# Latent norm and rotary steps on PSUM sources, the second attention's projections ahead, and levels 1 to 4 of a blocked triangular inverse on 32x32 blocks

## The reference

```python
x = x + 0.5 * swiglu(rms_norm(x, ffa_norm), ffa_w_in, ffa_w_out)
h = rms_norm(x, mix_norm)
c_q, c_kv, k_rope, g_q, g_k, g_v, g_b, g_a, g_z, m_qkv, gate_logits = split_cols(h @ w_in, IN_SPLITS)
# mla: latent norm, up projections, norm of each head, rotary turn, causal attention
q = rms_norm((rms_norm(c_q, cq_norm) @ w_uq).reshape(b, s, 8, 96), q_norm)
kv = (rms_norm(c_kv, ckv_norm) @ w_ukv).reshape(b, s, 8, 128)
# gdn: short convolution, l2 norm, then in chunks of 64 a unit lower triangular solve
sol = triangular_solve(eye + a, rhs, lower=True, unit_diagonal=True)
# moba: the second attention, 8 heads of 64
q = rope(rms_norm(q, q_norm), pos); k = rope(rms_norm(k, k_norm), pos)
x = x + sum(sigmoid(gate_logits) * (branches @ w_branch)) @ w_out
x = x + 0.5 * swiglu(rms_norm(x, ffb_norm), ffb_w_in, ffb_w_out)
```

## Time and profile before

| | |
|---|---|
| median of 3 runs | 2693.65 us (2691.25 to 2694.6) |
| the profiled execution | 2696.59 us, span 2694.8 us |
| PE busy | 2490.3 us, 92% of the span |
| DVE, ACT, POOL busy | 903.2, 901.4, 1022.9 us |
| mean granted TensorE clock | 0.965 |
| layer 1 | some 1166 to 1928 us of the span |
| layer 2 | some 1928 to 2692 us of the span |

### The profile page before, as it was taken

The page is one execution under the profiler, slowest core; times in us unless marked ns, Lnnn a source line. Parts: engine busy times, 40 slices in busy tenths (PEclk is TensorE's granted clock), DMA queues, the critical chain, the costliest instruction groups (busy, mean ns, idle before and its releaser), DMA issues. The chain is left out here.

```text
span 2694.8 us, 37867 instructions
## 1 busy us (share of the span) xinstructions
PE 2490.3 (92%) x15110; PEld 1793.4 (67%) x15110; DVE 903.2 (34%) x1374; ACT 901.4 (33%) x1310; POOL 1022.9 (38%) x428
## 2 busy tenths in 40 slices
PE   8879999999999999869998899899699988999999
PEld 3544443443343344349987799799699877998998
DVE  0331221221221122152147765321331287563211
ACT  1212111111111111134446533444344466523443
POOL 0000000000000000038866445688488675437786
PEclk9979999999999999879999899999899998999999
DMA  8139999999999999535544233455355443224453
GB/s 353 63 149 424 428 428 427 428 428 427 428 428 428 428 428 428 224 119 193 186 143 141 83 110 119 141 192 184 122 199 185 150 144 126 94 79 165 164 186 135
DMA packets 95100, 653.78 MB, mean 243 GB/s; under 512 B 10544, under 2 KB 12768, under 8 KB 68992
## 3 DMA queue, kind: packets, MB, share of 16 engines
q1 hardware_dynamic: 94976, 652.06, 62.8%
HBM read 650.96 MB, written 1.06 MB: 242 GB/s over the span
## 5 line engine op out<-in xcount | busy, mean ns | idle before, releaser
L502 POOL TENSOR_TENSOR w_lo<-raw,w_hi 128x1024 fp32r<-128x1024 f32 (+2 forms) x424 | 1022.7, 2437 | 1654.7 <-ACT w_hi L496 1654.7
L1764 PE MATMUL bank<-ring,scratch 128*64 128x512 f32 x3072 | 686.1, 596 | 28.6 <-DMA ring<-in_expert_units 26.3
L515 PE MATMUL bank<-hT_hi,w_hi 128*128 128x256 f32 x1984 | 568.7, 287 | 18.4 <-issue 13.4
L496 ACT CAST w_hi<-raw 128x1024 fp32r<-128x1024 f32 (+2 forms) x424 | 421.3, 1039 | 477.1 <-PE bank L517 440.0
L516 PE MATMUL bank<-hT_lo,w_hi 128*128 128x256 f32 x1984 | 565.0, 285 | 0.0
L517 PE MATMUL bank<-hT_hi,w_lo 128*128 128x256 f32 x1984 | 564.9, 285 | 0.0
L1764 PEld LDWEIGHTS bank<-ring,scratch 128*64 128x64 f32 x3072 | 209.5, 137 | 456.7 <-issue 387.0
L515 PEld LDWEIGHTS bank<-hT_hi,w_hi 128*128 128x128 f32 x1984 | 384.3, 194 | 21.3 <-issue 17.0
L516 PEld LDWEIGHTS bank<-hT_lo,w_hi 128*128 128x128 f32 x1984 | 384.2, 194 | 1.2 <-issue 0.5
L517 PEld LDWEIGHTS bank<-hT_hi,w_lo 128*128 128x128 f32 x1984 | 383.9, 194 | 0.0
L1932 DVE TENSOR_TENSOR scratch<-bank,scratch 128x512 f32<-128x512 f32 x64 | 44.3, 692 | 605.9 <-PE bank L1778 602.0
(11 more groups left out here) (309 smaller groups left out, 2803.0 us busy)
## 6 DMA issues: line engine op xcount, KB each, us to landing
ring<-in_expert_units SPq DMA_DIRECT2D x192, 2048.0 KB, 20.6
raw<-in_layer_halves SPq DMA_DIRECT2D x408, 512.0 KB, 4.1
ring<-in_first_units SPq DMA_DIRECT2D x6, 2048.0 KB, 24.1
ring<-in_ple_units SPq DMA_DIRECT2D x2, 2048.0 KB, 9.8
raw<-in_layer_halves SPq DMA_DIRECT2D x8, 424.0 KB, 3.4
scratch<-in_norm_gains SPq DMA_DIRECT2D x6, 512.0 KB, 5.2
raw<-in_layer_halves SPq DMA_DIRECT2D x4, 384.0 KB, 3.3
const<-in_const SPq DMA_DIRECT2D x1, 1184.0 KB, 7.3
```

The lines of the kernel that those rows point to most:

```text
L496: k.nc.scalar.copy(k.w[0][i % SPLIT_SLOTS][:, at], k.raw[n % RAW_SLOTS][:, 0:at.stop - at.start]).then_inc(k.sem("weights_hi"), 1)
L502: k.nc.gpsimd.tensor_tensor(k.w[1][i % SPLIT_SLOTS][:, at], k.raw[n % RAW_SLOTS][:, 0:at.stop - at.start], k.w[0][i % SPLIT_SLOTS][:, at], ...
L515: nc.tensor.matmul(out, lhsT[0], rhs[0], start=start, stop=False)
L1764: last = nc.tensor.matmul(b[g * SL:(g + 1) * SL, :], lhsT[:, c, :], w[:, c, g, :], start=start and c == 0, stop=stop and c == 3)
```

## The change

- **Latent norm.** DVE no longer copies the `mla` rows to SBUF. ACT squares from the bank, and DVE scales and copies from the bank; only 8 columns are still copied (`G.ab`). The weight slot of `("mla", 0)` is given back after its last product, not with `("mla", 1)`.
- **Rotary steps.** Three banks (2, 6, 7) are lent to DVE (`lend`, `borrow`): the tables are copied into one, the products x1 s1 and x2 s2 go to the other two, so that each tensor_tensor of `rope_dve` has one source in SBUF and one in PSUM. `moba` is done in two groups, q and k.
- **Order.** `moba` q and k are projected before `raw(0,1)`; their norms and rotary steps follow those of `mla` at once on DVE, and three waits for a root (`head_root_act`) now stand between ACT's casts. `z` 0 comes before `values_pe`, `gates(1,3)` after the second `out_turned_pe`.
- **Inverse.** In levels 1 to 4 the inverse has only 32x32 blocks on its diagonal. `Xc` and `XTc` hold these blocks side by side, 32 columns a head; a level is 8 products m_block Xc with 32 columns, a mask that spreads them to 128, 8 products with XTc, a subtract and a 32x32 block transpose on DVE (no `XP`). One of the four parts of `gates(2,0)`, 12 matmuls of 256 columns, stands between `P` and `PX` of each. Level 4 ends with a spread and a transpose to full size; levels 5 and 6 are as before. `first_level_pe` and `first_level_act` go.

```diff
-MIX_HALVES = [("mla", 0), ("mla", 1), ("gdn", 1, 0), ("gdn", 1, 1), ("gdn", 0, 0), ("up", 0), ("up", 1), ("gdn", 0, 1),
-              ("moba", 0, 0), ("moba", 0, 1), ("moba", 1, 0), ("moba", 1, 1), ("gdn", 2, 0), ("gdn", 2, 1),
+MIX_HALVES = [("mla", 0), ("mla", 1), ("gdn", 1, 0), ("gdn", 1, 1), ("gdn", 0, 0), ("up", 0), ("up", 1),
+              ("moba", 0, 0), ("moba", 0, 1), ("moba", 1, 0), ("moba", 1, 1), ("gdn", 0, 1), ("gdn", 2, 0), ("gdn", 2, 1),
...
+def rope_tables_to_bank(k, dve, link, a):
+
+    b, full, _free = k.borrow(dve, ("rope", a.n, 0))
+    dve.wait_ge(k.sem("rope_tables"), a.n + 1)
+    words = 4 * 2 * NT * a.half
+    k.nc.vector.tensor_copy(b[:, 0:words], a.flat).then_inc(full, 1)
...
+    c1, s2, c2, s1 = (bc(table[:, j, r0:r1].unsqueeze(2), [P, r1 - r0, H, a.half]) for j in range(4))
+    first = V_.tensor_tensor(tmp[0], x1, s1, ALU.mult)
+    second = V_.tensor_tensor(tmp[1], x2, s2, ALU.mult)
...
+def compact_pe(k, pe, lev, between):
...
+        for h in range(GH):
+            last = nc.tensor.matmul(b[:, h * BLOCK:(h + 1) * BLOCK], G.m_block[:, t, h, :], G.Xc[:, GH * t + h, :], start=True, stop=True)
...
+    next(between)
...
+        for h in range(GH):
+            last = nc.tensor.matmul(b[:, h * BLOCK:(h + 1) * BLOCK], G.P[:, t, h, :], G.XTc[:, GH * t + h, :], start=True, stop=True)
...
+def compact_dve(k, dve, link, lev):
...
+        V_.tensor_tensor(grid(G.P[:, t]), spread(part(b, GH, BLOCK)), bc(level, [P, GH, P // BLOCK, BLOCK]), ALU.mult).then_inc(free, 1)
...
+        V_.tensor_tensor(G.XTc[:, at], G.XTc[:, at], part(b, GH, BLOCK), ALU.subtract).then_inc(free, 1)
+        k.evacuated(dve, ("PX", lev, t))
+        if lev < COMPACT:
+            V_.transpose(G.Xc[:, at].rearrange("p a n -> p (a n)"), G.XTc[:, at].rearrange("p a n -> p (a n)")).then_inc(k.sem("x_turned"), 1)
+        else:
+            link(V_.tensor_tensor(grid(G.XT[:, t]), spread(G.XTc[:, at]), block_mask(G), ALU.mult))
+            V_.transpose(G.X[:, t].rearrange("p h n -> p (h n)"), G.XT[:, t].rearrange("p h n -> p (h n)")).then_inc(k.sem("x_turned"), 1)
...
-            whole(raw_pe(k, pe, 0, 1), moba_part[0])
-            next(moba_part[1])
+            whole(moba_part[0], moba_part[1], raw_pe(k, pe, 0, 1))
             transposed_pe(k, pe, mla)
...
-            for lev in range(1, LEVELS):
+            between = gates_pe(k, pe, 2, 0)
+            for lev in range(1, COMPACT + 1):
+                compact_pe(k, pe, lev, between)
+            for lev in range(COMPACT + 1, LEVELS):
                 level_pe(k, pe, lev)
-            whole(gates_pe(k, pe, 2, 0))
...
-            whole(*[gates_pe(k, pe, 1, q) for q in range(4)])
+            whole(*[gates_pe(k, pe, 1, q) for q in range(3)])
             out_turned_pe(k, pe, 1)
+            whole(gates_pe(k, pe, 1, 3))
...
-                    ins = V_.tensor_scalar(cn[:, t, c0:c1], rows[:, t, c0:c1], latent[:, i, t:t + 1], None, ALU.mult)
+                    ins = V_.tensor_scalar(cn[:, t, c0:c1], b[:, c0:c1], latent[:, i, t:t + 1], None, ALU.mult)
...
+            rope_tables_to_bank(k, dve, link, mla)
+            rope_dve(k, dve, link, mla, 0)
+            rope_tables_to_bank(k, dve, link, moba)
+            for g in range(2):
+                head_variance_dve(k, dve, link, moba, g)
+                head_scale_dve(k, dve, link, moba, g)
+                rope_dve(k, dve, link, moba, g)
```

More of the change, by code:

```diff
@@ new lines, in rope_tables_to_bank, with rope_dve @@
+def rope_tables_to_bank(k, dve, link, a):
[3 more added lines that the diff above has]
+    k.nc.vector.tensor_copy(b[:, 0:words], a.flat).then_inc(full, 1)
+    dve.wait_ge(full, k.uses.at["rope", a.n, 0][1] + 1)
+def rope_dve(k, dve, link, a, g):
+    V_, (r0, r1) = k.nc.vector, a.groups[g]
+    table = k.bank[k.uses.at["rope", a.n, 0][0]][:, 0:4 * 2 * NT * a.half].rearrange("p (j r f) -> p j r f", j=4, f=a.half)
+    if g == 0:
+        lent = [k.borrow(dve, ("rope", a.n, 1 + j)) for j in range(2)]
+    tmp = [k.bank[k.uses.at["rope", a.n, 1 + j][0]][:, :].rearrange("p (r h f) -> p r h f", h=H, f=a.half) for j in range(2)]
+    rows = a.qk.rearrange("p (r h) d -> p r h d", h=H)[:, r0:r1]
+    x1, x2 = rows[:, :, :, a.rope_at:a.rope_at + a.half], rows[:, :, :, a.rope_at + a.half:a.rope_at + 2 * a.half]
+    c1, s2, c2, s1 = (bc(table[:, j, r0:r1].unsqueeze(2), [P, r1 - r0, H, a.half]) for j in range(4))
+    first = V_.tensor_tensor(tmp[0], x1, s1, ALU.mult)
+    second = V_.tensor_tensor(tmp[1], x2, s2, ALU.mult)
+    if g == 0:
+        for j, ins in enumerate((first, second)):
+            ins.then_inc(lent[j][1], 1)
+    V_.tensor_tensor(x1, x1, c1, ALU.mult)
+    last = V_.tensor_tensor(x2, x2, c2, ALU.mult)
+    if g == len(a.groups) - 1:
+        last.then_inc(k.bank_free[k.uses.at["rope", a.n, 0][0]], 1)
+        k.evacuated(dve, ("rope", a.n, 0))
+    else:
+        link(last)
+    third = V_.tensor_tensor(x1, x1, tmp[1], ALU.subtract)
+    fourth = V_.tensor_tensor(x2, x2, tmp[0], ALU.add)
+    if g == len(a.groups) - 1:
+        third.then_inc(k.bank_free[k.uses.at["rope", a.n, 2][0]], 1)
+        fourth.then_inc(k.bank_free[k.uses.at["rope", a.n, 1][0]], 1)
+    else:
+        fourth.then_inc(k.sem("qk_ready"), 1)
@@ new lines, in lower_dve @@
+    for q in range(P // BLOCK):
+        at = slice(q * BLOCK, (q + 1) * BLOCK)
+        ins = V_.tensor_tensor(G.XTc[at], G.m.rearrange("p t h n -> p (t h) n")[at, :, at],
+                               bc(first[at, at].unsqueeze(1), [BLOCK, NT * GH, BLOCK]), ALU.mult)
+    link(ins)
+    link(V_.tensor_tensor(G.XTc, bc(G.identc.unsqueeze(1), [P, NT * GH, BLOCK]), G.XTc, ALU.subtract))
+    V_.transpose(G.Xc.rearrange("p a n -> p (a n)"), G.XTc.rearrange("p a n -> p (a n)")).then_inc(k.sem("x_turned"), 1)
@@ L2045, in layer_uses @@
     turned = [("qkT", q, t, half) for q, t in QKT for half in range(2)]
-    add(*[(("qkT", 0) + key[1:], b) for key, b in zip(turned, (2, 6, 7, 3, 4, 2, 6, 7))])
+    add(*[(("qkT", 0) + key[1:], b) for key, b in zip(turned, (1, 3, 4, 5, 1, 3, 4, 5))])
+    add((("raw", 2, 0), 1))
     add((("score", 0, 0, 0), 3), (("score", 0, 0, 1), 4))
-    add(*[(("score", 0, 1, g), b) for g, b in enumerate((2, 6, 7, 3))])
-    add((("raw", 2, 0), 1), (("raw", 2, 1), 4))
-    add((("pT", 0, 0, 0), 5), (("pT", 0, 0, 1), 0), (("ss",), 2), (("moba", 2, 0), 6), (("moba", 2, 1), 7))
@@ L2058, in layer_uses @@
-    add((("gates", 0, 0), 0), (("gates", 0, 1), 1))
+    add(*[(("score", 0, 1, g), b) for g, b in enumerate((5, 2, 6, 7))])
+    add((("raw", 2, 1), 0), (("moba", 2, 0), 3), (("moba", 2, 1), 4))
+    add((("pT", 0, 0, 0), 5), (("pT", 0, 0, 1), 2), (("ss",), 6))
+    add(*[(("pT", 0, 1, g), b) for g, b in enumerate((7, 5, 2, 7))])
+    add((("z", 0), 1), (("z", 1), 0), (("oT", 0, 0), 5), (("oT", 0, 1), 2))
+    add(*[(("qkT", 1) + key[1:], b) for key, b in zip(turned, (7, 6, 3, 4, 7, 6, 3, 4))])
@@ L2140, in _ @@
                         lnorm_pe(k, pe, 1, 1)
+                    if t == 1 and h == 0:
+                        last.then_inc(k.sem("half_used"), 1)
                 last.then_inc(full, 1)
```

257 lines of the change are left out of this document (141 added, 116 removed).

## The result

The changed kernel takes 2651.13 us, the median of 4 runs (2647.76 to 2652.72), where the kernel before takes 2693.94 us beside it. The ratio is 0.9839, 95% interval 0.9826 to 0.9851: 43 us less, where 37 were forecast. The profiled execution took 2647.76 us, the fastest of the four, with a span of 2645.6 us; against the 2694.8 us of before that is 49 us, so a sum of parts from the traces runs some 3 us a layer above what the medians say.

What follows compares the result with a forecast made beforehand. PE, busy 92% of the span, bounds the kernel, through waits, half clock and work. Terms summed to -18.5 us a layer, -37 for two: 2696.6 to 2659.6 us, median 2.9 lower, 2656.7 us; range 2638 to 2682 us.

Steps and rivals of the forecast that it cites:

- start: Latent norm up to the up projections: waits of 1.58 and 5.49 us and 2.1 us of half clock go; -9.2 us.
- middle: First attention's rotary steps and roots: 6.3 us of waits go, new waits of 2.9 and 5.0 and 1.7 clock come; +3.3 us.
- second attention's rotary steps: Ahead of the second attention's transposes: the 9.06 us wait and its half clock go, one wait grows; -9.9 us.
- inverse and clock in it, with the turning: Compact levels 1 to 4, levels 5 and 6, saved turning of `X`: -5.8 us; a third of compact levels' time lost to clock: +6.6.
- end: After the second `out_turned_pe`: `gates(1,3)` covers the turned output's way over ACT and DVE; -3.5 us.
- Right in both waits: PE's waits of 1.58 us for a weight half and 5.49 us ahead of the up projections were to go.
- The two new waits: PE was to wait 2.9 us for `moba(1,1)`'s weights and some 5 us for ACT to empty the first turned bank.
- The one more half-clock stretch: In the middle, the new waits of 3 and 5 us were to bring one more stretch at half clock, +1.7 us.
- as slow with PSUM as now: Rival: rotary operations gain nothing from PSUM, about 13 us return on DVE, PE sees perhaps 8; 2673 us, chance 0.05.
- the wait that was to grow from 1.26 to 2.5 us: PE's wait in the second attention, as ACT takes `moba` 2 ahead of the last probabilities' copies; about 2.5 us.
- the waits behind level 4: Inverse: PE waits for each tile's spread and full-size transpose, and for a POOL piece; +3.0 us.
- products which bring few columns cost the clock: In the four compact levels, few-column products lower PE's clock as waits do; +6.6 us, bounds 0 and +19.9.

Runs made afterwards that it cites:

- start_alone: Kernel before with only the latent-norm part of the change and `gate_logits_dve` moved behind `cT`; 2682.75 us, ratio 0.9948.
- copies_first: Changed kernel with ACT's copies of the first attention's turned q and k ahead of a convolution tap and two weight casts; 2644.04 us.
- cast_first: Changed kernel with the cast of `moba(1,1)`'s weights ahead of the decay's exponentials and the first root on ACT; 2652.53 us.
- sbuf_rotary: Changed kernel with rotary tables read from SBUF and the first attention's products kept in SBUF too; 2684.87 us, ratio 0.9953.
- wide_products: Changed kernel with each product in levels 1 to 4 moving 128 columns, its head's 32 four times over; 2639.93 us.
- wide_lengths: Changed kernel with the 16 products of `lengths_pe` moving 128 columns of ones instead of two; 2654.17 us.
- gates_behind: Changed kernel with all four parts of `gates(2,0)` behind level 6 instead of one in each compact level; 2652.54 us.
- gate_after_level4: Changed kernel with the fourth part of `gates(2,0)` moved from the middle of level 4 to behind its last product; 2642.53 us.
- old_end: Changed kernel with all four `gates(1,q)` parts ahead of the second `out_turned_pe` again; 2658.64 us, ratio 0.9853.

## Why the prediction came out right, and where it was off

The measured terms are of layer 2, from the starts of the stages' first matmuls in the two traces. In the middle the one block of 5.5 us that came from the next stretch, half of the second attention's v, is counted where it was.

| term | forecast | measured |
|---|---|---|
| start | -9.2 | -10.2 (47.19 to 36.97 us) |
| middle | +3.3 | -0.2 |
| second attention's rotary steps | -9.9 | -10.9 |
| inverse and clock in it, with the turning | -5.8 + 6.6 = +0.8 | +0.05 (+0.90 - 0.85) |
| end | -3.5 | -4.0 |
| sum | -18.5 | -25.2 |

**Start.** Right in both waits: L2455 at 0.47 us, and nothing ahead of the up projections. `start_alone` shows the term by itself. The cause is right in the main: scaling and copying `cn` and the rotary columns took DVE 12.4 us before and 2.1 us now. The 3.9 us of the moved `gate_logits_dve` were not in the prediction, and no run has the one without the other.

**Middle.** This is the term that was mis-sized, by 3.5 us. The two new waits came as described, behind the first root and behind the third. The `w_lo` wait was 2.38 us for 2.9. The wait for ACT was 2.74 us for "some 5 us". Its chain was right: from the second root to the third 8.84 us (forecast 9), then a tap and a cast, 2.9 us (forecast 3). But the second root came 8.1 us before the end of `raw(0,1)` and not 6, and that shortened the wait. L819 was taken at 3.36 us and took 4.49. The one more half-clock stretch came as forecast: the changed kernel has two of 3.4 us between the decay and the scores, the kernel before has one. `copies_first` and `cast_first` show that both waits hang on the roots in ACT's queue.

**Rotary steps.** Right. L841 to L854 take 0.68 to 0.70 us; the wait that was to grow from 1.26 to 2.5 us came to 1.74. `sbuf_rotary` shows what they would cost otherwise: the rival "as slow with PSUM as now" put it at 2673 us, and the run took 2685. That number is not the price of the rotary steps alone, since 9.2 us a layer of it, nearly all clock, lie in the inverse, which the rival did not have.

**Inverse.** PE's timeline at the start of level 1, eight products `P` (16 records) and the first gate matmul behind them:

```profile
2309.25 1.87 PE L1309 MATMUL bank<-scratch,h_rows 128*128 128x32 f32 x16
2310.95 0.36 PE L528 MATMUL bank<-hT_hi,w_hi 128*128 128x256 f32 x1
```

A product of 32 columns starts 0.21 us after the last (8 in 1.70 us), as the row with 2 columns had said; a level took 5.01 us (forecast 5.0); the subtract and the transpose took 0.28 and 0.31 us (taken at 0.25 each); the waits behind level 4 came to 2.3 us (forecast 3.0). These products show as two records each, 0.106 us apart. The 25 ns that the Trainium skill lists for matmuls of up to 64 columns ("TensorE: Matmul & The Clock Gate", section "Back-to-back issue gap") do not describe them; the same section says that this gap leaves the weight loads out.

**Clock.** The reason given, that products which bring few columns cost the clock though PE is never idle, was right: `wide_products` and `wide_lengths` took the loss away where they widened the products, and `gates_behind` made it worse. That the size came out near is luck in two ways. The stage's 38.77 us are 20.2 for four levels at full clock, 9.2 for levels 5 and 6, 0.8 for the tail's step, 2.3 of waits, and 6.2 that are left for the clock (forecast 6.6). But the 6.6 were a third of the compact levels' 20 us, and these lost only 3.2: levels 3 and 4 took 13.3 us without the wait, for 10.1 at full clock. The other 3.0 were lost behind the two waits, where levels 5 and 6 and the tail's step took 13.0 us for 10.0. The sum had those at full clock. `gate_after_level4` ran them at 0.99, without the waits; `wide_products` ran them at 1.00 in layer 1 and at 0.88 in layer 2, with the waits. Second, the prediction assumed one value for a kernel. From the first product of level 1 to the end of the tail's step the clock was at half for 13.7 us in the changed kernel, 17.1 in `cast_first`, 23.9 in `wide_lengths`, 13.7 and 27.3 in the two layers of `old_end`, and 34.1 in `sbuf_rotary`. That code is the same in all of them. What decides between these values stays open.

**End.** Right, with 3.46 us of wait back in `old_end`. The 0.5 us beyond the forecast are half clock at the transposes of the next norm, which the edit did not touch.

**The sum.** Layer 2 gained 6.7 us more than forecast in the profiled execution, over half of it in the middle, and layer 1, which went from 760.5 to 737.7 us from start to start, 4.3. That execution was the fastest of its four, and the median gained 6 us less than it.
